# A diffusion trunk with experts: weight rows read in pieces of 8 KB

## The chip, the cores and the metric

The kernel runs on one core of a Trainium2 chip. The metric is the time on the device in microseconds, the median of several executions. Before the change it is 2671.46 us (three runs, 2670.12 to 2673.77).

## The reference

Two layers of a diffusion backbone work on 512 latent tokens and 256 context tokens of width 1024, all in float32. A layer first mixes tokens in four parallel branches, and then sends each token through two of 16 experts. The change lies in this second half:

```python
h2 = modulate(rms_norm(x, norm2_g[i]), m[:, 3], m[:, 4])
x = x + m[:, 5] * grouped_moe(h2, router_w, router_b, moe_w1[i], moe_w3[i], moe_w2[i])
...
def grouped_moe(h, router_w, router_b, w1, w3, w2):
    logits = jnp.einsum('bld,de->ble', h, router_w, preferred_element_type=jnp.float32)
    ...
    for e in range(N_EXPERTS):
        a = jax.nn.silu(h @ w1[e]) * (h @ w3[e])
        y = y + combine[..., e:e + 1] * (a @ w2[e])
    return y
```

`w1[e]` and `w3[e]` are 1024 x 256, `w2[e]` is 256 x 1024: 1 MiB each; `combine` holds for each token the weights of its two experts, both of one group, and zeros. Layer 0 treats 768 tokens, layer 1 only the 512 latent ones.

## The kernel before, in words

There are 128 partitions (P), and D = 1024 = KD x P with KD = 8. Each engine has its own program; semaphores order them. The order of the work is written out by hand.

**Modulation.** The kernel begins with 48 slabs of 1 MiB of the modulation matrices, which SyncE loads into six slots (five in RING, one in HTF), each partition in eight pieces of 1 KB. During this time GpSimd loads constants, among them `rwv`, the router weights.

**Mixers.** For each layer there follow attention, the gating MLP, the convolution, the pooling and the output projection, in matmuls of L569 and L571. SyncE loads their weights into RAWB; ScalarE and VectorE split them into two parts.

**Router.** When the last column chunk of the output projection is in `x_t`, VectorE makes the modulated tokens, one tile of 128 tokens at a time: L1626 multiplies by the inverse norm and the gain, L1627 adds the shift, both over 128 x 1024 elements, into one of three buffers `h2tok`. Layer 0 has six tiles, layer 1 four. Of each tile ScalarE stores the rows to `h2_rows` in HBM (L1218). TensorE transposes it in eight pieces of 128 columns (L838, into `psb`), ScalarE copies the result to `h2T` (L1222), and eight products with the router weights `rwv[:, k, :]` follow (L846). TensorE takes the tiles in turn: transposes of tile t + 1, then the products of tile t. Piece k of a tile holds the columns k x 128 to k x 128 + 127, and `rwv` partition p holds rows k x 128 + p.

Then VectorE picks the experts in some 40 short instructions. Three of them (L1642, L1643, L1644) add pairs of the four scores of each group and write them to a table that has six columns for each group: L1642 writes runs of three elements, L1643 runs of two, L1644 single elements, so that the runs of one instruction lie 24 B apart. Products on TensorE give each token its place (L858 to L868). The result is a list of blocks: 27 blocks of 128 rows in layer 0 and 23 in layer 1, each with one expert (`eid_i`), and for each block the tokens that it gathers (`tab_i`).

**Experts.** For block b:

- GpSimd gathers 128 rows of `h2_rows` into `xg[b % 2]` (L1888), two blocks ahead; TensorE transposes them in eight pieces (L877) and ScalarE copies the result to `xgT` (L1240).
- SyncE loads three slabs of 1 MiB, `w1`, `w3` and `w2` of the block's expert, into the next of the six slots (L466), as soon as the slot is released (`slab_used`). In `w1` and `w3` partition p receives the rows p, p + 128, ..., eight pieces of 1 KB; in `w2` the rows p and p + 128, two pieces of 4 KB.
- TensorE multiplies (L885): for both matrices the sum over k of `xgT[:, k, :]` by `slot[:, k, :]`, 128 x 256 results each.
- ScalarE applies the silu to the first (L1236), VectorE multiplies it by the second into `act_a` (L1723), TensorE transposes `act_a` in two pieces (L901), and ScalarE copies them to `act_T` (L1244).
- TensorE multiplies by `w2` (L894), one block later; VectorE copies the result out (L1729), and ScalarE stores it to `y_rows` (L1249).

TensorE's order for a block is: L885 of block b, L877 of block b + 1, L894 of block b - 1, L901 of block b. After the last block GpSimd waits for the stores and gathers each token's two rows from `y_rows` (L1910); before it, it has issued the parameter loads of the next layer (L1808 to L1823).

Of the kernel before, what the change touches and what calls it, by code (L numbers as in the profile page):

```python
# [21 lines left out]
ALU = mybir.AluOpType  # L22
# [3 lines left out]
P = 128  # L26
D = 1024
KD = D // P
# [31 lines left out]
FF = 256  # L60
# [83 lines left out]
def trunk(nc, A, out):  # L144
# [7 lines left out]
    with ExitStack() as ctx:  # L152
# [3 lines left out]
        def place(name, width, dt=F32, parts=P, over=None):  # L156


            at_ = free[0] if over is None else over
            if over is None:  # L160
                free[0] += (width + 7) // 8 * 8
            return nc.alloc_sbuf_tensor_at(name, [parts, width], dt, offset=base + 4 * at_)
# [25 lines left out]
        rst = place("rst", 2 * AT)  # L188
# [15 lines left out]
        def W(l):  # L204
            return TOK if l < DEPTH - 1 else SEQ
# [4 lines left out]
        x_t = X[:, :].rearrange("p (t d) -> p t d", t=AT)  # L210
# [27 lines left out]
        def slot(s):  # L238
            return RING[:, s * SLAB:(s + 1) * SLAB] if s < SLOTS - 1 else HTF[:, 8 * D:8 * D + SLAB]
# [4 lines left out]
        def psb(i):  # L244
            return ps[:, i, :]
# [63 lines left out]
        mrow = HTF[:, 0:4 * D].rearrange("p (v m d) -> p v m d", v=2, m=2)  # L309
        gain2 = HTF[:, 4 * D:5 * D]  # L310
        grow = T[:, 0:2 * D].rearrange("p (v d) -> p v d", v=2)
        h2tok = [BRA[:, j * D:(j + 1) * D] for j in range(3)]
# [6 lines left out]
        sil = [late[:, 2 * D + j * FF:2 * D + (j + 1) * FF] for j in range(2)]  # L319
        act_a = [late[:, 2 * D + (2 + j) * FF:2 * D + (3 + j) * FF] for j in range(2)]  # L320
# [45 lines left out]
        rwv = rw[:, :].rearrange("p (k e) -> p k e", k=KD)  # L366
# [16 lines left out]
        def S(name):  # L383
            if name not in sems:
                sems[name] = ctx.enter_context(nc.semaphore(name))
            return sems[name]

        def at(name, l, n):

            return n + (signals(name) if l else 0)  # L390
# [64 lines left out]
        @block.sync  # L455
        def _(sp):
            issued = [0]

            def load(shape, src, before=None, at=None):

                n = issued[0] if at is None else at
                if n >= SLOTS or before is not None:
                    need = n - SLOTS + 1
                    sp.wait_ge(slab_used, need if before is None else before + need)
                a, m = shape
                sp.dma_start(slot(n % SLOTS)[:, 0:a * m].rearrange("p (a m) -> p a m", a=a), src)\  # L466
                    .then_inc(slab_full[n % SLOTS], 16)
                if at is None:
                    issued[0] += 1


            def mod_cols(l, c0):
                return A["mod_w"][l][:, c0].rearrange("(k p) n -> p k n", p=P)

            for j in range(SLOTS):
                load((KD, 256), mod_cols(0, slice(j * 256, (j + 1) * 256)))
            for l in range(DEPTH):
                start = 1 if l == 0 else 0
                turn0 = l * MC // 2
                with sp.Fori(start, MC // (2 * SLOTS)) as i:  # L480
                    for j in range(SLOTS):
                        load((KD, 256), mod_cols(l, bass.ds(i * (256 * SLOTS) + j * 256, 256)), i * SLOTS, turn0 + j)
                issued[0] = (l + 1) * MC // 2

            for l in range(DEPTH):

                if l == 0:
                    sp.wait_ge(S("mod_row"), DEPTH * MC // 2)
                else:
                    sp.wait_ge(S("y_sb"), at("y_sb", l - 1, expert_blocks(W(l - 1))))  # L490
                for r, pieces in enumerate(loads[l]):
                    if RAWS <= r < FIRST + 1:
                        sp.wait_ge(S("w_lo"), at("w_lo", l, r - RAWS + 1))
                    elif FIRST + 1 <= r < FIRST + RAWS:
                        sp.wait_ge(S("up_sb"), at("up_sb", l, up_items(l, AT)))
                    elif r >= FIRST + RAWS:
                        sp.wait_ge(S("w_lo"), split_no(l, r - FIRST - RAWS))
                    for o, a, m, src in pieces:
                        sp.dma_start(raw_slab(r, RAW)[:, o:o + a * m].rearrange("p (a m) -> p a m", a=a), src)\
                            .then_inc(raw_full[r % RAWS], 16)  # L500
                nb = expert_blocks(W(l))
                w1, w3, w2 = A["moe_w1"][l], A["moe_w3"][l], A["moe_w2"][l]

                sp.wait_ge(S("eid"), at("eid", l, 1))

                def up(b, n, before=None):
                    e = sp.value_load(eid_i[0:1, b] if before is None else eid_i[0:1, bass.ds(b, 1)],
                                      min_val=0, max_val=NE - 1)
                    for w in (w1, w3):
                        load((KD, FF), w[bass.ds(e, 1)].rearrange("e (k p) n -> p (e k) n", p=P), before, n)  # L510
                        n = None if n is None else n + 1

                def down(b, n, before=None):
                    e = sp.value_load(eid_i[0:1, b] if before is None else eid_i[0:1, bass.ds(b, 1)],
                                      min_val=0, max_val=NE - 1)
                    load((2, D), w2[bass.ds(e, 1)].rearrange("e (k p) n -> p (e k) n", p=P), before, n)

                up(slice(0, 1), None)

                sp.wait_ge(S("idx"), at("idx", l, 2))  # L520
                for b in (1, 2):
                    up(slice(b, b + 1), None)
                    down(slice(b - 1, b), None)
                n0 = issued[0]
                with sp.Fori(0, (nb - 3) // 2) as i:
                    for j in range(2):
                        up(i * 2 + (3 + j), n0 + 3 * j, i * SLOTS)
                        down(i * 2 + (2 + j), n0 + 3 * j + 2, i * SLOTS)
                issued[0] += 3 * (nb - 3)
                down(slice(nb - 1, nb), None)  # L530

            sp.wait_ge(S("x_stored"), 16 * LT)
# [750 lines left out]
        def _(dve):  # L1283
            chain = [0]

            def link(ins):

                chain[0] += 1
                ins.then_inc(S("dve_chain"), 1)
                dve.wait_ge(S("dve_chain"), chain[0])  # L1290

            tt, ts, stt, cp = dve.tensor_tensor, dve.tensor_scalar, dve.scalar_tensor_tensor, dve.tensor_copy
# [15 lines left out]
            for l in range(DEPTH):  # L1308
                n = l * MC // 2
# [48 lines left out]
            for l in range(DEPTH):  # L1358
# [104 lines left out]
                for n in range(len(steps) + 3):  # L1463
                    if n < len(steps):
                        h, t = steps[n]
# [12 lines left out]
                    if 2 <= n <= len(steps) + 1:  # L1478
                        m = n - 2
                        h, t = steps[m]  # L1480
# [4 lines left out]
                    if n >= 3:  # L1485
                        m = n - 3
                        h, t = steps[m]
# [46 lines left out]
                for c in range(BC):  # L1534
                    w = 3 * c + 2
# [39 lines left out]
                for g in range(BC):  # L1575
# [5 lines left out]
                    src, lo, k = pp[g % 2], 1, 1  # L1581
# [3 lines left out]
                    while 2 * k < win_:  # L1585
                        link(tt(pacc[1 - cur][:, lo + k:hi - k], pacc[cur][:, lo:hi - 2 * k], pacc[cur][:, lo + 2 * k:hi], ALU.add))
                        cur, lo, hi, k = 1 - cur, lo + k, hi - k, 2 * k
                    s_ = pacc[cur]
                    e = edge[:, (BC - 1 - g) * 2 * PP:(BC - g) * 2 * PP]
                    for a, b, o in pstreams:  # L1590
                        n = b - a
# [29 lines left out]
                for t in range(NT):  # L1621
                    v = 0 if t < LT else 1
                    if t >= 3:
                        dve.wait_ge(S("h2_tr"), at("h2_tr", l, t - 2))
                        dve.wait_ge(S(f"h2_st{t % 3}"), at(f"h2_st{t % 3}", l, 16 * (t // 3)))
                    link(stt(h2tok[t % 3], x_t[:, t, :], rst[:, t:t + 1], mrow[:, v, 1, :], ALU.mult, ALU.mult))  # L1626
                    tt(h2tok[t % 3], h2tok[t % 3], mrow[:, v, 0, :], ALU.add).then_inc(S("h2_tok"), 1)  # L1627


                s, sbv, m_, sc = (a[:, 0:NT, :] for a in (r_s, r_sb, r_m, r_sc))  # L1630
# [88 lines left out]
                def hidden(b, j, first=False):  # L1719
                    dve.wait_ge(S("sil"), at("sil", l, b + 1))  # L1720
                    if not first:
                        dve.wait_ge(S("aT_ps"), at("aT_ps", l, b - 1))
                    tt(act_a[j], sil[j], psb(1)[:, FF:2 * FF], ALU.mult).then_inc(S("a_sb"), 1)  # L1723

                def rows_out(b, j, stored=None):
                    dve.wait_ge(S("y_ps"), at("y_ps", l, b + 1))
# [21 lines left out]
                for t in range(NT + 3):  # L1748
                    if t < NT:
                        v = 0 if t < LT else 1  # L1750
# [12 lines left out]
        def _(pool):  # L1763
            chain = [0]

            def link(ins):

                chain[0] += 1
                ins.then_inc(S("pool_chain"), 1)
                pool.wait_ge(S("pool_chain"), chain[0])  # L1770
# [11 lines left out]
            for l in range(DEPTH):  # L1782
                for v in range(2):
                    pool.dma_start(mod_sb[l][v:v + 1, :], A["mod_b"][l].rearrange("(a n) -> a n", a=1)).then_inc(S("mod_b"), 16)
            pool.dma_start(rwv, A["router_w"].rearrange("(k p) e -> p k e", p=P)).then_inc(S("const_dma"), 16)
            pool.dma_start(rbias[:, :], A["router_b"].rearrange("(a e) -> a e", a=1).partition_broadcast(P)).then_inc(S("const_dma"), 16)
            pool.dma_start(edge[:, :], A["edges"].rearrange("g e -> (g e)").rearrange("(a n) -> a n", a=1).partition_broadcast(P))\
                .then_inc(S("const_dma"), 16)
# [47 lines left out]
            for l in range(DEPTH):  # L1836
# [67 lines left out]
                for t in range(NT):  # L1904
                    j = t % 3
# [29 lines left out]
```

## Time and profile before

| | |
|---|---|
| median of three runs | 2671.46 us (2670.12 to 2673.77) |
| span of the profiled execution | 2674.0 us; no time beside its span is given |
| TensorE matmuls busy | 2344.6 us, 88% |
| TensorE weight loads busy | 1882.4 us, 70% |
| VectorE busy | 1057.0 us, 40% |
| ScalarE busy | 746.3 us, 28% |
| DMA | 397.74 MB in 358022 packets |
| expert weights, SyncE's queue | 150 loads of 1024 KB, 7.5 us from issue to landing (median) |

The page gives for each engine the busy time and, in 40 equal slices of the span, its busy share in tenths. The stretches of the expert stages are about 1240 to 1560 us (layer 0) and 2370 to 2644 us (layer 1). The busy end of a matmul is modelled, so what TensorE waits for is read from the chain of waits and from the idle time that the timeline prints in brackets, with what ended it.

### The profile page before, as it was taken

How to read it: one execution, taken by the hardware profiler on the slowest of the kernel's cores; microseconds unless marked ns; L12 is line 12 of the kernel's file. 1: busy time of each engine (PE TensorE's matmuls, PEld its weight loads, DVE VectorE, ACT ScalarE, POOL GpSimd, SP SyncE). 2: the span in 40 equal slices, each digit the busy share in tenths (PEclk: the TensorE clock that was granted, in tenths of full speed). 3: DMA queues.
4: the chain of work that ended last, by engine and by line, in shares of the span. 5: the costliest groups of instructions: out<-in, count | busy, mean ns of one | idle time of the engine just before them, and what ended most of it. 6: DMA issues, size and time to landing. Idle time of an engine off the chain costs nothing.

```text
span 2674.0 us, 31031 instructions
## 1 busy us (share of the span) xinstructions
PE 2344.6 (88%) x12289; PEld 1882.4 (70%) x12289; DVE 1057.0 (40%) x1455; ACT 746.3 (28%) x1086; POOL 152.8 (6%) x231
## 2 busy tenths in 40 slices
PE   6877599999999999976999936599999999869995
PEld 4555478888888888865777725388878777657773
DVE  5782777213224243232111153675243454321113
ACT  4552444214112122231111132443232222311111
POOL 1010200000000000000101120200000000001111
PEclk9988799999999999987999977799999999879998
DMA  9970100122122223215999971100233433269996
GB/s 329 355 236 1 48 1 1 44 55 71 48 60 76 59 68 99 81 57 196 361 369 364 368 279 34 47 1 24 76 94 83 110 91 127 83 227 365 366 367 227
DMA packets 358022, 397.74 MB, mean 149 GB/s; under 512 B 9852, under 2 KB 319260, under 8 KB 356892
## 3 DMA queue, kind: packets, MB, share of 16 engines
q1 hardware_dynamic: 331264, 297.56, 35.8%
q0 software_dynamic: 14272, 53.63, 5.6%
q10 hardware_dynamic: 12384, 45.09, 4.2%
q8 instruction: 75, 1.23, 0.2%
q14 instruction: 27, 0.22, 0.0%
HBM read 359.45 MB, written 36.80 MB: 148 GB/s over the span
## 4 chain that ended last, share of the span: by engine, by line
PE 56%; DVE 6%; ACT 2%; issue 1%; DMA 1%; POOL 0%; POOLq 0%; DVEq 0%; ACTq 0%
PE ps L569 22%; PE ps L885 13%; PE ps L894 6%; PE ps L571 4%; PE ps L559 3%; PE ps L877 2%; PE ps L741 2%; PE ps L730 1%; PE ps L846 1%; DMA MGZ<-y_rows,slot_i 1%; ACT BR L1213 0%; DVE X L1392 0%; PE ps L901 0%; PE ps L838 0%; PE ps L700 0%
## 5 line engine op out<-in xcount | busy, mean ns | idle before, releaser
L569 PE MATMUL ps<-HTH,WS 128*128 128x512 f32 x1664 | 581.2, 396 | 15.1 <-issue 7.3
L569 PEld LDWEIGHTS ps<-HTH,WS 128*128 128x128 f32 x1664 | 314.2, 189 | 88.5 <-issue 9.9
L569 PE MATMUL ps<-HTL,WS 128*128 128x512 f32 x832 | 327.6, 394 | 0.0
L1420 DVE TENSOR_TENSOR WS<-RAWB,WS 128x1024 fp32r<-128x1024 f32 (+1 forms) x128 | 190.5, 1490 | 222.7 <-ACT WS L1071 222.3
L885 PE MATMUL ps<-RING,MGZ 128*128 128x256 f32 x1216 | 275.9, 384 | 2.8 <-ACT MGZ L1240 2.8
L885 PEld LDWEIGHTS ps<-RING,MGZ 128*128 128x128 f32 x1216 | 232.5, 193 | 35.4 <-ACT MGZ L1240 3.9
L1071 ACT ACTIVATE WS<-RAWB 128x1024 fp32r<-128x1024 f32 (+1 forms) x128 | 162.6, 1272 | 263.0 <-PE ps L571 133.3
L571 PE MATMUL ps<-HTH,WS 128*128 128x256 f32 x832 | 233.2, 280 | 0.0
L569 PE MATMUL ps<-BRH,WS 128*128 128x512 f32 x512 | 183.2, 396 | 6.5 <-DVE BRL L1572 3.6
L569 PEld LDWEIGHTS ps<-HTL,WS 128*128 128x128 f32 x832 | 157.2, 189 | 36.0 <-issue 0.7
L894 PE MATMUL ps<-RING,MGZ 128*128 128x512 f32 x392 | 176.4, 593 | 0.5 <-ACT MGZ L1244 0.5
L1437 DVE TENSOR_TENSOR T<-T,ps 128x768 f32<-128x768 f32 (+1 forms) x48 | 39.4, 820 | 312.7 <-PE ps L571 202.0
L1723 DVE TENSOR_TENSOR MGZ<-MGZ,ps 128x256 f32<-128x256 f32 x50 | 21.1, 421 | 348.5 <-ACT MGZ L1236 348.5
L571 PEld LDWEIGHTS ps<-HTH,WS 128*128 128x128 f32 x832 | 157.5, 189 | 0.1
L1089 ACT ACTIVATE T<-ps 128x768 f32<-128x768 f32 (+1 forms) x64 | 45.1, 705 | 302.8 <-PE ps L571 190.0
L559 PE MATMUL ps<-MODH,scH 128*2 128x256 f32 x384 | 110.0, 286 | 21.3 <-DVE MODL L1301 20.3
L1729 DVE COPY MGZ<-ps 128x1024 f32<-128x1024 f32 x50 | 61.2, 1224 | 170.4 <-PE ps L894 170.4
L894 PEld LDWEIGHTS ps<-RING,MGZ 128*128 128x128 f32 x392 | 70.7, 190 | 71.0 <-issue 70.3
L569 PEld LDWEIGHTS ps<-BRH,WS 128*128 128x128 f32 x512 | 96.7, 189 | 30.1 <-DVE BRL L1572 4.8
L571 PE MATMUL ps<-HTL,WS 128*128 128x256 f32 x416 | 116.3, 280 | 0.0
L1236 ACT ACTIVATE MGZ<-ps 128x256 f32<-128x256 f32 x50 | 19.2, 384 | 334.6 <-PE ps L885 334.6
L559 PE MATMUL ps<-MODL,scH 128*2 128x256 f32 x384 | 109.9, 286 | 0.0
(295 smaller groups left out, 3892.8 us busy)
## 6 DMA issues: line engine op xcount, KB each, us to landing
RING<-in_moe_w SPq DMA_DIRECT2D x125, 1024.0 KB, 7.5
RAWB<-in_w_in SPq DMA_DIRECT2D x112, 512.0 KB, 3.9
RING<-in_mod_w SPq DMA_DIRECT2D x40, 1024.0 KB, 11.7
HTF<-in_moe_w SPq DMA_DIRECT2D x25, 1024.0 KB, 7.4
y_rows<-MGZ ACTq DMA_DIRECT2D x50, 512.0 KB, 6.9
RAWB<-in_w_branch SPq DMA_DIRECT2D x64, 256.0 KB, 4.4
HTF<-in_mod_w SPq DMA_DIRECT2D x8, 1024.0 KB, 11.8
RAWB<-in_w_o SPq DMA_DIRECT2D x16, 512.0 KB, 3.6
```

What stands on the lines that cost most here:

```text
L559: last = mm(out, a, b, start=(first and i == 0), stop=(stop and i == 2))
L569: last = mm(psb(pair)[:, 0:SEQ], a[:, k0 + k, :], b[:, k, 0:SEQ], start=go, stop=end)
L571: last = mm(psb(pair)[:, SEQ:TOK], a[:, k0 + k, :], b[:, k, SEQ:TOK], start=go, stop=end)
L741: last = mm(psb(3)[0:VD, (m % 2) * P:(m % 2 + 1) * P], vb[:, kt, h * VD:(h + 1) * VD], prT[m % 2][:, kt * P:(kt + 1) * P], start=(kt == ks ...
L877: last = pe.transpose(psb(0)[:, k * P:(k + 1) * P], xg[j][:, k * P:(k + 1) * P], ident[:, :])
L885: last = mm(psb(1)[:, o:o + FF], xgT[j][:, k, :], slot3(s, KD)[:, k, :], start=(k == 0), stop=(k == KD - 1))
L894: last = mm(psb(2 + j)[:, n * 512:(n + 1) * 512], act_T[j][:, k, :], w[:, k, n * 512:(n + 1) * 512], start=(k == 0), stop=(k == 1))
L1071: act_f(parts(s, words(s))[0], raw_slab(r, words(s)), ACT.Copy).then_inc(S("w_hi"), 1)
L1089: act_f(sig[u % 2][:, 0:W(l)], psb(u % 2)[:, 0:W(l)], ACT.Sigmoid).then_inc(S("g_sig"), 1)
L1420: tt(lo, raw_slab(FIRST + s, words(s)), hi.bitcast(F32), ALU.subtract).then_inc(S("w_lo"), 1)
L1437: link(tt(prod[:, 0:W(l)], sig[u % 2][:, 0:W(l)], psb(2 + u % 2)[:, 0:W(l)], ALU.mult))
L1729: cp(ysb[j], psb(2 + j)).then_inc(S("y_sb"), 1)
```

## The change

Partition p of the expert weights now receives consecutive rows: the rows 8p to 8p + 7 of `w1` and `w3`, and the rows 2p and 2p + 1 of `w2`. Both are one piece of 8 KB for each partition. What is multiplied by them must stand in the same order: piece k of a tile of tokens must hold the columns 8p + k. For this L1626 and L1627 write column 8p + k to place k x 128 + p; what they read from `x_t` and `mrow` stays in order, and L1627 reads its first operand where it writes it. `h2_rows` and the gathered rows then have this order without more work. The router weights are loaded in it too. L1723 does the same for `w2` with two pieces.

```diff
@@ experts, SyncE @@
                     for w in (w1, w3):
-                        load((KD, FF), w[bass.ds(e, 1)].rearrange("e (k p) n -> p (e k) n", p=P), before, n)
+                        load((KD, FF), w[bass.ds(e, 1)].rearrange("e (p k) n -> p (e k) n", p=P), before, n)
...
-                    load((2, D), w2[bass.ds(e, 1)].rearrange("e (k p) n -> p (e k) n", p=P), before, n)
+                    load((2, D), w2[bass.ds(e, 1)].rearrange("e (p k) n -> p (e k) n", p=P), before, n)
@@ tokens, VectorE @@
-                    link(stt(h2tok[t % 3], x_t[:, t, :], rst[:, t:t + 1], mrow[:, v, 1, :], ALU.mult, ALU.mult))
-                    tt(h2tok[t % 3], h2tok[t % 3], mrow[:, v, 0, :], ALU.add).then_inc(S("h2_tok"), 1)
+                    by_row = h2tok[t % 3].rearrange("q (k p) -> q p k", k=KD)
+
+                    def rows_of(a):
+                        return a.rearrange("q (p k) -> q p k", k=KD)
+
+                    link(stt(by_row, rows_of(x_t[:, t, :]), rst[:, t:t + 1], rows_of(mrow[:, v, 1, :]), ALU.mult, ALU.mult))
+                    tt(by_row, by_row, rows_of(mrow[:, v, 0, :]), ALU.add).then_inc(S("h2_tok"), 1)
@@ gated product, VectorE @@
-                    tt(act_a[j], sil[j], psb(1)[:, FF:2 * FF], ALU.mult).then_inc(S("a_sb"), 1)
+                    tt(act_a[j].rearrange("q (k p) -> q p k", k=2), sil[j].rearrange("q (p k) -> q p k", k=2),
+                       psb(1)[:, FF:2 * FF].rearrange("q (p k) -> q p k", k=2), ALU.mult).then_inc(S("a_sb"), 1)
@@ constants, GpSimd @@
-            pool.dma_start(rwv, A["router_w"].rearrange("(k p) e -> p k e", p=P)).then_inc(S("const_dma"), 16)
+            pool.dma_start(rwv, A["router_w"].rearrange("(p k) e -> p k e", p=P)).then_inc(S("const_dma"), 16)
```

## Rows read from the trace of the kernel before

**Rows 1.** The page: TensorE's busy time; DMA share and rate in 40 slices.

```profile
PE 2344.6 (88%) x12289; PEld 1882.4 (70%) x12289; DVE 1057.0 (40%) x1455; ACT 746.3 (28%) x1086; POOL 152.8 (6%) x231
...
DMA  9970100122122223215999971100233433269996
GB/s 329 355 236 1 48 1 1 44 55 71 48 60 76 59 68 99 81 57 196 361 369 364 368 279 34 47 1 24 76 94 83 110 91 127 83 227 365 366 367 227
```

**Rows 2.** The page: the chain of waits, share of the span by line.

```profile
PE ps L569 22%; PE ps L885 13%; PE ps L894 6%; PE ps L571 4%; PE ps L559 3%; PE ps L877 2%; PE ps L741 2%; PE ps L730 1%; PE ps L846 1%; DMA MGZ<-y_rows,slot_i 1%; ACT BR L1213 0%; DVE X L1392 0%; PE ps L901 0%; PE ps L838 0%; PE ps L700 0%
```

**Rows 3.** The chain in order of time (start us, us), layer 0's experts.

```profile
1269.89 6.91 PE ps L885 x32
...
1532.93 6.91 PE ps L885 x32
```

**Rows 4.** Waits of SyncE's queue, 1269 to 1537 us: total, times, longest.

```profile
SPq L466 <- PE ps L901: 76.9, 24, 3.3
```

**Rows 5.** DMA, 130 to 155 us: modulation slabs in pieces of 1 KB.

```profile
DMA packets 8633, 8.70 MB, mean 348 GB/s; under 512 B 136, under 2 KB 8633, under 8 KB 8633
```

**Rows 6.** DMA, 1525 to 1562 us: rate in 40 slices, packets by size.

```profile
GB/s 403 421 412 360 376 369 343 348 356 369 384 381 394 421 412 421 443 412 430 412 412 403 406 318 188 177 319 421 415 328 241 98 0 0 244 403 407 80 0 0
DMA packets 4621, 11.77 MB, mean 318 GB/s; under 512 B 432, under 2 KB 2512, under 8 KB 4365
```

**Rows 7.** TensorE's timeline (start, us, [idle before]), start of both expert stages.

```profile
1243.79 1.94 PE L877 MATMUL ps<-ident,BR 128*128 128x128 f32 x8 [6.10 <-DMA BR<-h_rows,idx_i]
1246.84 9.36 PE L885 MATMUL ps<-RING,MGZ 128*128 128x256 f32 x32 [1.11 <-ACT MGZ L1240]
...
2375.47 9.95 PE L885 MATMUL ps<-RING,MGZ 128*128 128x256 f32 x32 [1.11 <-ACT MGZ L1240]
```

**Rows 8.** By stretch: busy us by engine, granted clock (PEclk), DMA share, GB/s.

```profile
1246.80:1251.50 4.70, 4.66 (x11) 3.75 (x12) 0.00 (x0) 1.28 (x1) 0.97 (x1) 0.52 1.01 356
```

**Rows 9.** GpSimd's timeline, end of layer 0.

```profile
1566.14 1.06 POOL L1910 DMA_INDIRECT MGZ<-y_rows,slot_i  x1 [15.26 <-DMA y_rows<-MGZ]
```

**Rows 10.** Timelines of VectorE and TensorE in one block, 1400 to 1424 us.

```profile
1403.22 0.42 DVE L1723 TENSOR_TENSOR MGZ<-MGZ,ps 128x256 f32<-128x256 f32 x1 [6.49 <-ACT MGZ L1236]
...
1403.31 3.60 PE L894 MATMUL ps<-RING,MGZ 128*128 128x512 f32 x8
1406.75 0.38 PE L901 MATMUL ps<-ident,MGZ 128*128 128x128 f32 x2
```

**Rows 11.** TensorE's timeline, router: tiles 1, 2 and 5 of layer 0, tile 3 of layer 1.

```profile
1193.72 1.97 PE L838 MATMUL ps<-ident,BR 128*128 128x128 f32 x8 [0.47 <-DVE BR L1627]
...
1197.98 1.09 PE L838 MATMUL ps<-ident,BR 128*128 128x128 f32 x8
...
1206.60 1.09 PE L838 MATMUL ps<-ident,BR 128*128 128x128 f32 x8
...
2340.47 1.09 PE L838 MATMUL ps<-ident,BR 128*128 128x128 f32 x8
```

**Rows 12.** VectorE's timeline, tiles 2 and 5 of layer 0, tile 3 of layer 1.

```profile
1194.90 1.22 DVE L1627 TENSOR_TENSOR BR<-BR,HTF 128x1024 f32<-128x1024 f32 x1
...
1202.29 1.23 DVE L1627 TENSOR_TENSOR BR<-BR,HTF 128x1024 f32<-128x1024 f32 x1
...
2336.56 1.23 DVE L1627 TENSOR_TENSOR BR<-BR,HTF 128x1024 f32<-128x1024 f32 x1
```

**Rows 13.** VectorE's groups by form: count, busy us, mean ns, idle before.

```profile
L1627 DVE TENSOR_TENSOR BR<-BR,HTF 128x1024 f32<-128x1024 f32 x10 | 12.2, 1225 | 0.3
L1612 DVE TENSOR_TENSOR X<-X,ps 128x768 f32<-128x768 f32 x8 | 7.6, 954 | 46.5 <-PE ps L825 46.5
...
L1642 DVE TENSOR_TENSOR BR<-BR 128x72 f32<-128x72 f32 x1 | 0.2, 234 | 0.0
L1642 DVE TENSOR_TENSOR BR<-BR 128x48 f32<-128x48 f32 x1 | 0.2, 210 | 0.0
L1644 DVE TENSOR_TENSOR BR<-BR 128x24 f32<-128x24 f32 x1 | 0.2, 194 | 0.0
L1644 DVE TENSOR_TENSOR BR<-BR 128x16 f32<-128x16 f32 x1 | 0.2, 181 | 0.0
```

## The prediction

> **What bounds the kernel now.** I read the page first. TensorE is busy 88% of the span, and 16 DMA engines are nearly full in three stretches: the modulation matrices at the start and the expert stage of each layer [rows 1]. The change touches the expert stages, so the question is which of the two ends last there. The chain of waits over the whole span gives the expert lines L885 and L894 13% and 6% as TensorE work, and no weight load stands among its lines [rows 2].
>
> The slices show the difficulty: there the DMA engines are full too, at 361 to 369 GB/s in the whole slices. The chain in order of time settles it. One block of 128 rows is 32 matmuls of L885 and what follows them (8 transposes, 8 matmuls of L894, 2 transposes), and in the middle of layer 0's stage it comes back 23 times in (1532.93 - 1269.89)/23 = 11.44 us, each time the 6.91 us of L885 and no transfer between them [rows 3]. From the other side, SyncE waits on TensorE for a slab to be freed, 24 times and 76.9 us in the largest of three such groups [rows 4]; no row has TensorE waiting for a weight slab. So the loads are hidden, but only just: a block moves 3 MiB of weights, 0.5 MiB of gathered rows and 0.5 MiB of results, 4.19 MB in 11.44 us = 367 GB/s.
>
> **The loads: what 8 KB pieces change.** With nothing but 1 KB pieces the engines are full at about 348 GB/s: the modulation stage [rows 5]. Where 4 KB and 8 KB pieces mix with them, behind the last gather of layer 0 (256 packets of 8 KB are in that window), single slices run at 400 to 443 GB/s [rows 6]. Now half of a block's bytes (w1, w3) go in 1 KB pieces: 2.10 MB / 348 = 6.0 us; the other half in 4 KB pieces at some 410: 5.1 us; together 11.1 of the 11.44 us. After the change 4.19 MB / 410 = 10.2 us. The gain of 0.9 us a block is worth nothing, because TensorE's 11.44 us cover either number: 46 blocks in the steady state, 0 us. Were that cover gone, the 0.9 us would be worth 41 us. From the other side, a loss begins only where pieces of 8 KB flow at under 367 GB/s.
>
> The Trainium skill, "DMA: Bandwidth & Descriptors", section "Why small descriptors are slow (HBM only)", gives each packet about 3 extra bus cycles of 32 bytes. That is 35 against 32 for 1 KB and 259 against 256 for 8 KB, so by it 348 would become some 376 GB/s, an estimate from that page. The slices of [rows 6] already exceed it, and by either number the sum does not move.
>
> Where the loads are not in the steady state: block 0 of layer 0 starts at 1246.84, behind the first gather, its transposes and their copy. Its 9.36 us for 32 matmuls instead of 6.91 are the granted clock, 0.52 (the lower level, 1.2 GHz) up to 1251.5, and not a late slab; layer 1 has 9.95 us there [rows 7, 8]. TensorE does wait for the first gather, 6.10 us in layer 0 [rows 7]. Its packets come to an end while the next weight loads begin, and those now stand in front of it in 8 KB packets instead of 1 KB. 16 engines at 367 GB/s need 0.36 us for one, so one or two of them cost 0 to 0.7 us a layer; for two layers I take +0.4 us. It can gain no more than the same.
>
> At the end of a layer nothing is lost: after the next layer's parameter loads, which share the engines with the last weights, GpSimd still waits 15.26 us for the last results to be stored [rows 9], so they may land that much later. The router weights (512 B rows instead of 64 B) load during the modulation stage and L846 first reads them behind tile 1's transposes, after 1193.72 us [rows 11]: 0.
>
> **The gated product (L1723).** 50 instructions of 0.42 us, now written with a step of 512 B between consecutive elements. In the steady state it ends at 1403.64 and the transposes that read it start at 1406.75, behind the 3.6 us of L894 [rows 10]: 3.1 us of cover, seven times its length. Block 0 has no L894 in front, but there TensorE waits for ScalarE's copy of the next gathered rows anyway. I take 0. Without the cover even a doubling would cost 0.27 us x 50 = 13 us.
>
> **The tokens (L1626, L1627).** Here the change is on the path. These two instructions make one tile of h2. TensorE waits for the first two tiles of a layer (tile 1 of layer 0: 0.47 us) and for none after them: a tile takes TensorE (1206.60 - 1197.98)/3 = 2.87 us in L838 and L846, VectorE (1202.29 - 1194.90)/3 = 2.46 us [rows 11, 12]. From there to block 0 everything is a chain (router, one-hots, table, gather), so a delay of the last router matmul arrives in full. Let each of the two instructions become x longer. In layer 0 tile t is ready 2x(t+1) later. Tiles 0 and 1 have no slack; tile 2 has 1197.98 - 1196.12 = 1.8 us, and tile 5 has 1206.60 - 1203.52 = 3.0. The end is later by the largest of 4x (tile 1) and 12x - 3.0 (tile 5). In layer 1, with four tiles and 2340.47 - 2337.79 = 2.6 us of slack at tile 3, it is the largest of 4x and 8x - 2.6.
>
> What is x? No row has an instruction that steps by 512 B. The nearest are the pair sums of the router, whose results step by 24 B from one group to the next [rows 13]. Runs of three elements cost (234 - 210)/24 = 1.0 ns an element, as in contiguous rows, (1225 - 954)/256 = 1.06. Single elements cost (194 - 181)/8 = 1.63. The surplus of 0.57 ns over 1024 elements is x = 0.58 us. Below: x = 0, as stepping rows of three elements cost nothing. Above: a second full slot for each element, x = 1.09 us. I take 0.58, the row of single elements, as that is the new pattern. Then layer 0: max(2.3, 4.0) = 4.0; layer 1: max(2.3, 2.0) = 2.3. Sum with the gather: 4.0 + 2.3 + 0.4 = **+6.7 us**.
>
> The durations come from an execution with a span of 2674.0 us, for which no time beside its span is given; that is 0.1% above the median of 2671.46 of the three runs, to which I add the sum: 2678.2.
>
> **Rivals.**
> 1. *Stepping is free* (x = 0). For: the rows of three elements, and what L1626 only reads stays contiguous. Against: single elements differ. Sum 0 to +0.4: 2671.6 us.
> 2. *A full second slot*, x = 1.09: layer 0 13.1 - 3.0 = 10.1, layer 1 8.7 - 2.6 = 6.1, sum 16.6: 2688 us. For it speaks only that 512 B is far beyond 24 B. If only L1627, which also reads at that step, pays it, the sum is 3.5 + 2.2 + 0.4: 2677.6, beside my number for another reason. The Trainium skill, "Advanced Engine Details and Errata", section "SBUF Cachelines", says that full speed needs at least two accesses to the same line of 16 bytes; it names no price. The order of the two prices, for runs of three and for single elements, agrees with it; no row shows it at this step.
> 3. *Faster*: the start of the expert stage is waiting for weights after all, and block 0's surplus, 9.36 - 6.91 and 9.95 - 6.91, goes. That is 2.45 + 3.04 = 5.5 us, which with free stepping gives 2666. Against it stands the clock of 0.52 [rows 8]. It decides only if x is next to 0.
> 4. *Pieces of 8 KB are slower than 1 KB*, below 367 GB/s: each GB/s below costs 0.03 us a block; at the 348 of [rows 5] it is 12.0 - 11.44 = 0.6 us x 46 = +28 us: 2699. Against: the slices of [rows 6].
>
> **How the numbers follow.** 0.2% of this kernel, 5.3 us, is about what a measurement can tell from no change; x above about 0.5 passes it. Chances: my case (x from 0.3 to 0.8) 0.40, of it 0.30 above the bound and 0.10 within; free stepping 0.33; the second slot 0.17; faster 0.07; slower loads 0.03. Slower 0.30 + 0.17 + 0.03 = 0.50; same 0.10 + 0.33 = 0.43; faster 0.07. The range leaves out rivals 3 and 4 and a little of the edges: 2670 to 2689; my own case alone spans 2673 to 2682.
>
> **What the profile would show.** L1627 near 1.81 instead of 1.23 us and L1626 longer by as much; the waits of L838 on L1627 longer by 1 to 2 us; block 0 starting 4 us later in layer 0; L1723 perhaps longer without effect; the interval of 11.44 us unchanged; DMA packets down by 50 x 2048 x 7/8 and 50 x 128 = 96,000; a DMA share in the expert stage that falls from 1.03 to about 0.9. I am wrong if the interval moves, if L1627 keeps its 1.23 us, or if TensorE gets new idle time there that keeps its clock low for longer.

## The result, and the profile after

Compared in turns on one chip, the changed kernel took 2683.25 us (9 runs, 2678.72 to 2687.82) and the kernel before 2673.77 us (9 runs, 2670.12 to 2683.04): ratio 1.0031, 95% interval 1.0020 to 1.0042. By the ratio that is 8.3 us more (interval 5.3 to 11.2), where 6.7 were forecast. The median of the kernel before lay between 2673.8 and 2678.2 us over all comparisons, so below only the ratios of runs made together are compared.

First the groups of VectorE by form (count | busy us, mean ns | idle before) of the changed kernel; L1631, L1632 and L1728 are L1626, L1627 and L1723 of the kernel before. L1627 stands in [rows 13]; the first two lines here are the other two of the kernel before:

```profile
L1626 DVE SCALAR_TENSOR_TENSOR BR<-X,rst,HTF 128x1024 f32<-128x1024 f32 x10 | 12.8, 1280 | 0.1
L1723 DVE TENSOR_TENSOR MGZ<-MGZ,ps 128x256 f32<-128x256 f32 x50 | 21.1, 421 | 348.5 <-ACT MGZ L1236 348.5
...
L1728 DVE TENSOR_TENSOR MGZ<-MGZ,ps 128x256 f32<-128x256 f32 x50 | 30.4, 608 | 348.2 <-ACT MGZ L1236 348.2
L1631 DVE SCALAR_TENSOR_TENSOR BR<-X,rst,HTF 128x1024 f32<-128x1024 f32 x10 | 19.9, 1992 | 0.1
L1632 DVE TENSOR_TENSOR BR<-BR,HTF 128x1024 f32<-128x1024 f32 x10 | 19.2, 1918 | 0.3
```

L1632 is 1918 - 1225 = 693 ns longer than L1627, and L1631 is 1992 - 1280 = 712 ns longer than L1626. The gated product, 421 ns before, is 187 ns longer over 256 elements, 0.73 ns an element. So the step costs about 0.7 us in an instruction of 1024 elements.

What TensorE makes of it stands in its timeline, changed kernel, router of layer 0 and then layer 1 (start, us, idle before), to be held against [rows 11]:

```profile
1190.30 1.94 PE L838 MATMUL ps<-ident,BR 128*128 128x128 f32 x8 [13.85 <-DVE BR L1632]
1194.10 1.97 PE L838 MATMUL ps<-ident,BR 128*128 128x128 f32 x8 [1.86 <-DVE BR L1632]
...
1198.30 1.10 PE L838 MATMUL ps<-ident,BR 128*128 128x128 f32 x8
...
1201.86 1.10 PE L838 MATMUL ps<-ident,BR 128*128 128x128 f32 x8 [0.61 <-DVE BR L1632]
...
1205.72 1.09 PE L838 MATMUL ps<-ident,BR 128*128 128x128 f32 x8 [0.92 <-DVE BR L1632]
...
1209.60 1.09 PE L838 MATMUL ps<-ident,BR 128*128 128x128 f32 x8 [0.93 <-DVE BR L1632]
...
1215.17 0.54 PE L852 MATMUL ps<-ident,MGZ 16*128 16x16 f32 x6 [0.89 <-ACT MGZ L1224]
...
2339.28 1.97 PE L838 MATMUL ps<-ident,BR 128*128 128x128 f32 x8 [1.86 <-DVE BR L1632]
2341.18 3.20 PE L846 MATMUL ps<-MGZ,rw 128*16 128x128 f32 x16
...
2347.19 1.09 PE L838 MATMUL ps<-ident,BR 128*128 128x128 f32 x8
...
2352.55 0.42 PE L852 MATMUL ps<-ident,MGZ 16*128 16x16 f32 x4 [0.68 <-ACT MGZ L1224]
```

In layer 0 tiles 3, 4 and 5 now wait for VectorE, which they did not before: VectorE has become the slower of the two, at 3.9 us a tile. In layer 1 only tiles 0 and 1 wait. To measure the stage I take the reciprocal (L1620), which comes just before the first tile, as its start, and the transposes of the router's scores (L852) as its end. VectorE's rows of the changed kernel:

```profile
1186.09 0.19 DVE L1620 RECIPROCAL rst<-srt 128x6 f32<-128x6 f32 x1 [1.35 <-ACT srt L1215]
...
2331.27 0.18 DVE L1620 RECIPROCAL rst<-srt 128x4 f32<-128x4 f32 x1 [1.35 <-ACT srt L1215]
```

and five rows of the kernel before that are not shown above, VectorE's and TensorE's:

```profile
1188.44 0.19 DVE L1620 RECIPROCAL rst<-srt 128x6 f32<-128x6 f32 x1 [1.35 <-ACT srt L1215]
...
1212.18 0.54 PE L852 MATMUL ps<-ident,MGZ 16*128 16x16 f32 x6 [0.89 <-ACT MGZ L1224]
...
2327.66 0.18 DVE L1620 RECIPROCAL rst<-srt 128x4 f32<-128x4 f32 x1 [1.35 <-ACT srt L1215]
...
2334.83 2.84 PE L846 MATMUL ps<-MGZ,rw 128*16 128x128 f32 x16
...
2345.84 0.42 PE L852 MATMUL ps<-ident,MGZ 16*128 16x16 f32 x4 [0.68 <-ACT MGZ L1224]
```

Layer 0: (1215.17 - 1186.09) - (1212.18 - 1188.44) = 5.3 us. Layer 1: 21.28 - 18.18 = 3.1 us. Together 8.4 us, as much as the ratio gives (8.3 us).

These are rows of one execution each, and the granted clock does not rise at the same moment in all of them. The changed kernel once more (last experiment) shows it in the first products of layer 0:

```profile
1198.33 3.60 PE L846 MATMUL ps<-MGZ,rw 128*16 128x128 f32 x16
```

They take 3.60 us at a granted clock of 0.50, instead of 2.37 us at 0.79; tiles 3 and 4 then do not wait, and still its stage lasts 29.07 us, where the profile above has 29.08: VectorE sets the end. In executions where VectorE's instructions have their old length, TensorE sets it, and the stage of layer 0 lasts between 23.5 (2.17 us for these products) and 25.2 us (3.60 us). So the 5.3 us of layer 0 are known to about 1.5 us.

The loads did change. The chain of waits of the changed kernel, first and last of 24 blocks, and the table by stretch (busy us by engine, granted clock, DMA share, GB/s) show what became of it:

```profile
1284.56 6.91 PE ps L885 x32
...
1547.60 6.91 PE ps L885 x32
```

```profile
1280.00:1550.00 270.00, 270.00 (x1181) 202.52 (x1180) 44.00 (x48) 43.03 (x72) 34.16 (x60) 1.00 0.97 367
```

The interval is (1547.60 - 1284.56)/23 = 11.44 us, as in [rows 3]. The DMA engines move the same 367 GB/s with a share of 0.97 (about 0.9 was forecast), where the same stretch of the kernel before has 1.03:

```profile
1270.00:1540.00 270.00, 270.00 (x1185) 203.88 (x1184) 38.77 (x47) 41.52 (x71) 34.12 (x60) 1.00 1.03 366
```

The packets fell from 358,022 to 262,022, by the 96,000 of the forecast.

### The profile page after: what moved, and what is told of

It reads as the page before. It is cut to its first block, busy times and chain, and to the rows that moved or that the text cites. A ratio compares the mean times of both kernels' runs of the same rounds, so it can differ in the third digit from the quotient of the medians.

```text
span 2681.4 us, 31031 instructions
## 1 busy us (share of the span) xinstructions
PE 2344.2 (87%) x12289; PEld 1880.6 (70%) x12289; DVE 1080.1 (40%) x1455; ACT 746.6 (28%) x1086; POOL 152.4 (6%) x231
## 2 busy tenths in 40 slices
DMA packets 262022, 397.74 MB, mean 148 GB/s; under 512 B 9852, under 2 KB 216860, under 8 KB 241692
## 3 DMA queue, kind: packets, MB, share of 16 engines
q8 instruction: 75, 1.23, 0.2%
## 4 chain that ended last, share of the span: by engine, by line
PE 56%; DVE 7%; ACT 2%; issue 2%; DMA 1%; POOL 0%; POOLq 0%; DVEq 0%; ACTq 0%
PE ps L569 22%; PE ps L885 13%; PE ps L894 6%; PE ps L571 4%; PE ps L559 3%; PE ps L877 2%; PE ps L741 2%; PE ps L730 1%; DMA MGZ<-y_rows,slot_i 1%; DVE BR L1631 1%; PE ps L846 0%; ACT BR L1213 0%; DVE X L1392 0%; PE ps L901 0%; DVE BR L1632 0%
## 5 line engine op out<-in xcount | busy, mean ns | idle before, releaser
L885 PE MATMUL ps<-RING,MGZ 128*128 128x256 f32 x1216 | 276.5, 385 | 2.7 <-ACT MGZ L1240 2.7
L885 PEld LDWEIGHTS ps<-RING,MGZ 128*128 128x128 f32 x1216 | 233.0, 193 | 35.4 <-ACT MGZ L1240 3.7
L1728 DVE TENSOR_TENSOR MGZ<-MGZ,ps 128x256 f32<-128x256 f32 x50 | 30.4, 608 | 348.2 <-ACT MGZ L1236 348.2
L1735 DVE COPY MGZ<-ps 128x1024 f32<-128x1024 f32 x50 | 61.2, 1225 | 161.8 <-PE ps L894 154.9
```

The source lines that it names most:

```text
L885: last = mm(psb(1)[:, o:o + FF], xgT[j][:, k, :], slot3(s, KD)[:, k, :], start=(k == 0), stop=(k == KD - 1))
L1735: cp(ysb[j], psb(2 + j)).then_inc(S("y_sb"), 1)
```

## The experiments

**The loads alone.** The two lines of SyncE are changed, all else is the kernel before. The products then pair tokens and weights that do not belong together.

```diff
-  w[bass.ds(e, 1)].rearrange("e (k p) n -> p (e k) n", p=P)
+  w[bass.ds(e, 1)].rearrange("e (p k) n -> p (e k) n", p=P)      # w1, w3, and w2 likewise
```

> The kernel before with only SyncE's expert loads changed to 8 KB pieces (the products then pair tokens and weights in different orders). My theory: TensorE's 11.44 us per block hide them, so the interval stays 11.44 us, and the ratio to before is 1.000 within 0.0005. Rival (8 KB packets delay other traffic, such as the first gather or the stores, and this is part of the 0.31%): ratio above 1.001. Rival (a gain that the token part hides): below 0.999.

Ratio 0.9993, interval 0.9983 to 1.0003. The interval of a block is 11.44 us. In the table by stretch of this kernel the only clear difference is the DMA share, 0.98 instead of 1.03:

```profile
1270.00:1540.00 270.00, 270.00 (x1181) 202.41 (x1181) 38.27 (x47) 42.61 (x72) 34.10 (x60) 1.00 0.98 366
```

A gain of up to 0.17% is not excluded; a loss above 0.03% is. The loads carry none of the 0.31%.

**VectorE alone.** The changed kernel with the old loads (the diff above, backwards).

> The changed kernel with SyncE's expert loads put back to 1 KB and 4 KB pieces (the products then pair tokens and weights in different orders); the stepping writes of VectorE and the router weights stay. My theory: the whole loss is here, ratio to before 1.003 (1.002 to 1.004), L1631 at 1.99 us and L1632 at 1.92, router stage later by 5.3 us in layer 0 and 3 us in layer 1. Rival (the loads carry part of it): ratio 1.001 or less.

Ratio 1.0022, interval 1.0014 to 1.0031; the groups by form are those of the changed kernel:

```profile
L1631 DVE SCALAR_TENSOR_TENSOR BR<-X,rst,HTF 128x1024 f32<-128x1024 f32 x10 | 19.9, 1995 | 0.1
L1632 DVE TENSOR_TENSOR BR<-BR,HTF 128x1024 f32<-128x1024 f32 x10 | 19.2, 1921 | 0.3
```

The loss is here. The interval overlaps that of the whole change (1.0020 to 1.0042), and the stage, measured as above, lasts 29.12 us in layer 0 and 21.28 in layer 1, as in the changed kernel (29.08 and 21.28).

**The cover taken away.** Both kernels with half of the products of w1 and w3 left out; all loads stay.

```diff
-  for k in range(KD):
+  for k in range(KD // 2):
       last = mm(psb(1)[:, o:o + FF], xgT[j][:, k, :], slot3(s, KD)[:, k, :],
-                start=(k == 0), stop=(k == KD - 1))
+                start=(k == 0), stop=(k == KD // 2 - 1))
```

> The kernel before, with L885 summing only four of the eight pieces (half of the products of w1 and w3 are left out, all loads stay). TensorE then needs 11.44 - 16 x 0.216 = 8.0 us a block, and no longer covers the DMA engines. My theory, from 2.10 MB at 348 GB/s and 2.10 MB at 410: the interval becomes 11.1 us, set by the loads. Rival (1 KB pieces are not the limit and the engines follow TensorE): 8 to 10 us.

> The changed kernel with the same half of the products left out. My theory: interval 10.2 us (4.19 MB at 410 GB/s), 0.9 us a block less than with the small pieces, so 46 x 0.9 = 41 us less in the expert stages, and against the other kernel with half the products some 33 us after the loss of the tokens. Rival (packet size does not matter to these loads): the same interval in both.

Small pieces: ratio 0.9903 to the kernel before (0.9880 to 0.9927), median 2655.65 us. Pieces of 8 KB: 0.9717 (0.9701 to 0.9734), 2603.54 us. The first answer is that of the small pieces, TensorE's waits and the table by stretch, the second that of the 8 KB pieces:

```profile
PE ps L885 <- DMA RING<-in_moe_w: 45.5, 21, 4.0
...
1280.00:1500.00 220.00, 181.25 (x666) 123.16 (x667) 32.58 (x40) 35.41 (x59) 23.08 (x40) 0.90 1.06 380
```

```profile
PE ps L885 <- DMA RING<-in_moe_w: 45.2, 24, 6.7
...
1280.00:1500.00 220.00, 182.84 (x756) 124.39 (x757) 40.29 (x44) 39.38 (x66) 30.41 (x54) 1.00 1.02 422
```

Now L885 waits for the slabs in both, and the rate is what the DMA engines can give: 380 GB/s in small pieces, 422 in 8 KB pieces. With 4.19 MB that is 11.0 and 9.9 us a block (forecast 11.1 and 10.2). The 1.1 us a block, 51 us over 46 blocks, are the gain of the 8 KB pieces, and it appears only where TensorE does not cover it. Between the two medians lie 2655.65 - 2603.54 = 52 us, where 33 were forecast. The loss of the tokens, 8 us, is already taken off there, so the loads gave about 60 us, 9 more than the 51. The clock may be part of that: with small pieces TensorE was granted 0.90 in the stretch, with large ones 1.00. No run separates the two. Rival 4, slower large pieces, is out.

**Which step costs, in writes.** The changed kernel with the old loads and another permutation in each tile of layer 0, so that consecutive elements are written 8, 16, 32, 128, 512 and 2048 B apart in tiles 0 to 5. The columns stand in a wrong order.

```diff
-  by_row = h2tok[t % 3].rearrange("q (k p) -> q p k", k=KD)
+  kk = (512, 256, 128, 32, 8, 2)[t]
+  by_row = h2tok[t % 3].rearrange("q (k p) -> q p k", k=kk)      # and so in rows_of
```

> The changed kernel with the old loads, and with another step for the writes of the two token instructions in each tile: 8, 16, 32, 128, 512 and 2048 B for tiles 0 to 5 (the columns then stand in another order in each tile). Theory A (a write that does not stay in a 16 B line costs, whatever the step): 1.28 and 1.23 us at 8 B, 1.99 and 1.92 us at all steps from 16 B on. Theory B (the cost grows with the step, as the row at 24 B with 0.57 ns and the result at 512 B with 0.70 suggest): rising from 8 B to 2048 B. Theory C (only steps of large powers of two cost): full speed at 16 and 32 B.

VectorE's timeline, tiles 0 (8 B), 1 (16 B), 4 (512 B) and 5 (2048 B); in this kernel and the next, L1632 and L1633 are L1626 and L1627 of the kernel before:

```profile
1187.69 1.28 DVE L1632 SCALAR_TENSOR_TENSOR BR<-X,rst,HTF 128x1024 f32<-128x1024 f32 x1
1189.01 1.23 DVE L1633 TENSOR_TENSOR BR<-BR,HTF 128x1024 f32<-128x1024 f32 x1
1190.16 2.07 DVE L1632 SCALAR_TENSOR_TENSOR BR<-X,rst,HTF 128x1024 f32<-128x1024 f32 x1
1192.26 1.97 DVE L1633 TENSOR_TENSOR BR<-BR,HTF 128x1024 f32<-128x1024 f32 x1
...
1202.18 2.05 DVE L1632 SCALAR_TENSOR_TENSOR BR<-X,rst,HTF 128x1024 f32<-128x1024 f32 x1
1204.26 1.92 DVE L1633 TENSOR_TENSOR BR<-BR,HTF 128x1024 f32<-128x1024 f32 x1
1206.09 2.04 DVE L1632 SCALAR_TENSOR_TENSOR BR<-X,rst,HTF 128x1024 f32<-128x1024 f32 x1
1208.16 2.01 DVE L1633 TENSOR_TENSOR BR<-BR,HTF 128x1024 f32<-128x1024 f32 x1
```

Theory A holds: 8 B are free, 16 B cost the full price, and 2048 B no more. Tiles 2 and 3 (32 and 128 B) take 2.07 and 2.00 us in L1632, 2.02 and 2.09 in L1633. The price does not grow with the step, so 512 B was no special case. This is one execution, and the four tiles of its layer 1 repeat the first four within 0.02 us. All these steps are powers of two; others were not measured, but for the 24 B of the router's rows.

**Which step costs, in reads.** The same, walking in the written order: the writes are contiguous, L1632 reads two operands with the step, L1633 one (the shift; its other operand is contiguous).

```diff
+  kk = (2, 4, 8, 32, 128, 512)[t]
+  by_row = h2tok[t % 3].rearrange("q (k p) -> q k p", k=kk)      # and so in rows_of
```

> The same with contiguous writes and the steps in what is read, 2048, 1024, 512, 128, 32 and 8 B for tiles 0 to 5 counted by the elements of x and mrow: L1631 reads two stepping operands, L1632 one (columns in another order in each tile). Theory A (only writes pay): 1.28 and 1.23 us everywhere. Theory B (reads pay as writes do): 1.99 and 1.92 us for all but the 8 B tile, and more in L1631 if both operands count.

The expectation has the steps in the wrong order: they are 8, 16, 32, 128, 512 and 2048 B in tiles 0 to 5. Again this is one execution. Tiles 0, 1, 4 and 5:

```profile
1183.36 1.28 DVE L1632 SCALAR_TENSOR_TENSOR BR<-X,rst,HTF 128x1024 f32<-128x1024 f32 x1
1184.68 1.22 DVE L1633 TENSOR_TENSOR BR<-BR,HTF 128x1024 f32<-128x1024 f32 x1
1185.83 2.07 DVE L1632 SCALAR_TENSOR_TENSOR BR<-X,rst,HTF 128x1024 f32<-128x1024 f32 x1
1187.93 1.98 DVE L1633 TENSOR_TENSOR BR<-BR,HTF 128x1024 f32<-128x1024 f32 x1
...
1197.98 2.47 DVE L1632 SCALAR_TENSOR_TENSOR BR<-X,rst,HTF 128x1024 f32<-128x1024 f32 x1
1200.49 1.91 DVE L1633 TENSOR_TENSOR BR<-BR,HTF 128x1024 f32<-128x1024 f32 x1
1202.30 1.33 DVE L1632 SCALAR_TENSOR_TENSOR BR<-X,rst,HTF 128x1024 f32<-128x1024 f32 x1
1203.67 1.24 DVE L1633 TENSOR_TENSOR BR<-BR,HTF 128x1024 f32<-128x1024 f32 x1
```

Reads pay like writes from 16 B on. With two stepping operands L1632 takes 2.07, 2.10, 2.19 and 2.47 us at 16, 32, 128 and 512 B, so there the price does grow with the step. Tile 5 is the odd one: its walk takes one element here, one 2048 B further on, the next one here, and so on. Read in this way it costs almost nothing; written in the same way (tile 5 of the writes) it costs the full price.

**The step moved into the reads.** The same result as the changed kernel; `"q (k p) -> q k p"` and `"q (p k) -> q k p"` in the places of the patterns of the diff.

> The changed kernel with the same result, but each of the three instructions walks in the order in which it writes, so the writes are contiguous and the reads step (32 B in the tokens, 8 B in the gated product). If reads do not pay: L1631 and L1632 back at 1.28 and 1.23 us, ratio to before 1.000, 8 us less than the changed kernel. If they pay as writes do: ratio 1.003 as the changed kernel.

Ratio 1.0042, interval 1.0029 to 1.0056. L1631 and L1632 take 2094 and 2010 ns, more than with stepping writes; the gated product, which reads with a step of 8 B, is back at 421 ns. It is the expectation's second case. The stage lasts 30.30 us in layer 0 and 21.90 in layer 1, so in the trace it is somewhat worse than the changed kernel (29.08 and 21.28); the intervals of the two ratios overlap.

**One instruction instead of two.** L1633 (L1626 of the kernel before) writes contiguously to a free buffer, only L1634 writes with the step.

```diff
-  link(stt(by_row, rows_of(x_t[:, t, :]), rst[:, t:t + 1], rows_of(mrow[:, v, 1, :]), ALU.mult, ALU.mult))
-  tt(by_row, by_row, rows_of(mrow[:, v, 0, :]), ALU.add).then_inc(S("h2_tok"), 1)
+  if t:
+      dve.wait_ge(S("h2_tok"), at("h2_tok", l, t))
+  link(stt(junk, x_t[:, t, :], rst[:, t:t + 1], mrow[:, v, 1, :], ALU.mult, ALU.mult))
+  tt(by_row, rows_of(junk), rows_of(mrow[:, v, 0, :]), ALU.add).then_inc(S("h2_tok"), 1)
```

> The changed kernel with the same result, but L1631 writes contiguously to a buffer that is free at this time, and only L1632 writes with the step. L1631 back at 1.28 us, L1632 stays at 1.92; a tile costs 0.7 us more than before instead of 1.4. By the sum of the prediction: layer 0 max(1.4, 4.2 - 3.0) = 1.4, layer 1 max(1.4, 2.8 - 2.6) = 1.4, together 2.8 us: ratio to before 1.001. Rival (the read at the step of 512 B is what pays in L1632): L1632 back near 1.23 us and ratio 1.000.

```profile
L1634 DVE TENSOR_TENSOR BR<-BR,HTF 128x1024 f32<-128x1024 f32 x10 | 19.4, 1935 | 0.3
L1633 DVE SCALAR_TENSOR_TENSOR BR<-X,rst,HTF 128x1024 f32<-128x1024 f32 x10 | 12.8, 1285 | 0.7
```

Ratio 1.0016, interval 1.0004 to 1.0027: half of the cost, 4.3 us, where 2.8 were forecast. L1634 reads contiguously here and still takes 1935 ns, so the write alone costs the full price. The stage grows by 2.2 us in layer 0 and 2.4 in layer 1 instead of 1.4 each. What is beyond the forecast stands in the first products of each layer, which the sum had left out: they take 2.98 and 3.60 us, 2.42 and 2.84 before.

**Pairs.** As in the last one, but the walk of L1634 and of the gated product takes two elements in a row wherever it writes, and reads two lines by turns.

```diff
-  by_row = h2tok[t % 3].rearrange("q (k p) -> q p k", k=KD)
+  by_row = h2tok[t % 3].rearrange("q (k u i) -> q u k i", k=KD, i=2)
...
-      return a.rearrange("q (p k) -> q p k", k=KD)
+      return a.rearrange("q (u i k) -> q u k i", k=KD, i=2)
```

> The changed kernel with the same result and its 8 KB loads, but VectorE walks so that two elements in a row share a line of 16 B wherever it writes: L1633 goes contiguously to the free buffer, L1634 and the gated product write pairs (pairs 512 B apart), and read two lines by turns, one element of each. Theory (the price is for a write that has its line of 16 B alone, and reads of two lines by turns cost nothing, as tile 5 of the read steps with 1.33 and 1.24 us has it): L1634 near 1.25 us, gated product near 0.42 us, ratio to before 1.000, 8 us less than the changed kernel. Rival (any jump of 512 B costs, pair or not): L1634 near 1.6 to 1.9 us, ratio 1.001 to 1.002.

```profile
L1730 DVE TENSOR_TENSOR MGZ<-MGZ,ps 128x256 f32<-128x256 f32 x50 | 21.1, 422 | 348.7 <-ACT MGZ L1236 348.7
L1634 DVE TENSOR_TENSOR BR<-BR,HTF 128x1024 f32<-128x1024 f32 x10 | 12.4, 1238 | 0.3
```

Ratio 0.9996, interval 0.9987 to 1.0005: the same permutation, the same 8 KB pieces, and the cost is gone. The jump of 512 B is still there after each pair, and the instruction takes 1238 ns instead of 1225. (L1633 takes 1285 ns, as in the last experiment; the walk in pairs was not tried in it.)

**The step on TensorE.** Tokens and gated product stay in order as before; the transposes read with the step.

```diff
-  h2tok[t % 3][:, k * P:(k + 1) * P]
+  h2tok[t % 3].rearrange("q (p k) -> q k p", k=KD)[:, k, :]      # and so for xg (k=KD) and act_a (k=2)
```

> The changed kernel with the same result and its 8 KB loads, but tokens and gated product stay in plain order, VectorE as in the kernel before, and TensorE's transposes read with the step (32 B in L838 and L877, 8 B in L901). If TensorE's reads at a step are free: transposes at 0.11 us each, interval 11.44 us, ratio 1.000. If they pay as VectorE's do (0.7 of a slot per element): 10 transposes of some 0.11 us grow to 0.19 us, interval 12.2 us, +0.8 us x 48 = +38 us, ratio 1.014.

TensorE's timeline of this kernel, one block:

```profile
1409.87 1.05 PE L877 MATMUL ps<-ident,BR 128*128 128x128 f32 x8
...
1414.19 0.39 PE L901 MATMUL ps<-ident,MGZ 128*128 128x128 f32 x2
```

Ratio 0.9991, interval 0.9982 to 1.0000. The eight transposes of L877 take 1.05 us instead of 1.04, those of L838 1.16 instead of 1.09, and the interval of a block is 11.46 us. The step is not free for TensorE itself: it stands in the loads of the weights, which run beside the matmuls. TensorE's groups of weight loads, this kernel and then the kernel before (count, busy us, mean ns, idle before):

```profile
L877 PEld LDWEIGHTS ps<-ident,BR 128*128 128x128 f32 x416 | 55.5, 192 | 16.0 <-issue 13.3
...
L877 PEld LDWEIGHTS ps<-ident,BR 128*128 128x128 f32 x416 | 49.9, 144 | 17.1 <-issue 12.1
```

A load takes 192 ns instead of 144 with a step of 32 B, and 197 instead of 141 in L901 with a step of 8 B, but almost nothing of it reaches the time of the transposes.

**The changed kernel again**, with these last two:

> The changed kernel once more, on the same chip as the two others: ratio 1.003 as before, so that their differences are not those of a chip.

Ratio 1.0032, interval 1.0021 to 1.0042. Its interval does not touch those of the two versions that write in pairs or step on TensorE. Neither of these is shown to beat the kernel before: what they keep of the change, the faster loads, is covered.

## Why the prediction was right

- **The bound of the expert stage** was read rightly: the interval stayed at 11.44 us, the loads alone gave 0.9993, and with the cover gone they gave 1.1 us a block (0.9 forecast). Both were priced a little high: the small pieces at 11.1 us against 11.0, the large ones at 10.2 against 9.9.
- **The place of the loss** was right: L1626 and L1627 on the path, with two tiles without slack and the last tile deciding in layer 0.
- **x was sized too low**: 0.58 us, from two rows of single elements that differ by 13 ns, against 0.69 in L1632 and 0.71 in L1631. No row said that a price read at a step of 24 B would hold even roughly at 512 B. The write steps showed it only afterwards, so this part was luck. With 0.70 the formulas give 12 x 0.70 - 3.0 = 5.4 us for layer 0 (measured 5.3) and the larger of 4 x 0.70 = 2.8 and 8 x 0.70 - 2.6 = 3.0 for layer 1. In layer 1 3.1 us came, but by the other way: tile 3 does not wait, the products after tiles 0 and 1 start 2.7 us later and take 3.20 us instead of 2.84, the rest. They run while the granted clock changes between its levels; it was 0.57 over them, 0.66 before. The prediction named this effect and did not price it. That the longer wait in front keeps the clock low is not shown. In layer 1 the products take 3.17 to 3.21 us in three executions with this wait (1.86 us), and 2.81 to 2.91 in four with a wait of at most 0.60. But with a wait of 1.30 us (one instruction instead of two) they take 3.60, and with 2.07 (the step moved into the reads) 3.03.
- **The gather's +0.4 us is not seen.** TensorE waits 5.90 and 5.83 us for it, instead of 6.10 and 5.76. But the changed kernel again has 6.11 and 6.30, so single executions differ by more than the term, and no run shows it or excludes it.
- **The sum**: 4.0 + 2.3 + 0.4 = 6.7 us against 5.3 + 3.1 and no gather. The two layers were priced 2.1 us too low, and the unseen 0.4 hides a little of that. Of the 5 us between the 2678.2 that were forecast and 2683.25, 2.3 are the kernel before, which was measured at 2673.77 instead of 2671.46.
- **Rival 1**, free stepping, fell in its general form, but it is true for a step of 8 B and for pairs. **Rival 2**, a full second slot of 1.09 us, was too dear; the price is 0.7. **Rival 3** had no place: with 8 KB pieces the 32 matmuls of block 0 of layer 0 still take 9.80 us, with a granted clock of 0.50 over the first half.
- **The gated product** grew to 608 ns, as unimportant as was said: TensorE waits for it 0.23 us in block 0 of each layer, in place of a wait for ScalarE's copy.
- The Trainium skill, "Advanced Engine Details and Errata", section "SBUF Cachelines", asks for at least two accesses to a line of 16 B. For writes the runs agree: two to a line are enough (8 B step, pairs), one is not (16 B step and up). For reads they agree but for one kind: reads that change lines at every element and come back to both are nearly free (tile 5 of the read steps, 1.33 and 1.24 us; L1634 of the pairs, 1238 ns).
- The Trainium skill, "DMA: Bandwidth & Descriptors", section "Why small descriptors are slow (HBM only)", gave the estimate of 376 GB/s from 348. No run here has a stage of 8 KB weight pieces alone. The mixed stage went from 380 to 422, a factor of 1.11 where the estimate has 1.08 with all bytes in 1 KB pieces to begin with, so by the runs it is too small.

## What to carry to other kernels

Before a load is made faster, ask what covers it, and find the price of the order that it forces on others: here a covered gain of 1.1 us a block was bought with 0.7 us in instructions on the path. If a permutation must be made, walk so that elements are written in pairs of neighbours, or let TensorE's transpose read with the step; both took the loss away here, and neither made the kernel faster than before. And look at the pace of both engines in a pipeline of tiles: later tiles may have slack, but once the feeding engine becomes the slower one (3.9 us a tile against 2.87), each further tile adds.

## What had not been expected of the hardware

- VectorE's price for float32 writes at steps of 16, 32, 128, 512 and 2048 B is 0.67 to 0.84 ns an element and does not grow with the step (2.07 against 1.28 us and 1.97 against 1.23 at 16 B, 2.04 and 2.01 at 2048 B), and not a second slot of 1.06.
- Reads of two places by turns, 2048 B apart and each going on by 4 B, take 1.24 us instead of 1.22, writes of that kind 2.01: only the times are shown, the mechanism is not.
- Two operands read with a step of 512 B cost 2.47 us, one 1.91. Why these two lie further apart at 512 B than at 16 B (2.07 and 1.98) stays open.
- TensorE's weight loads do pay for a step, and at 8 B already, which is free on VectorE: 197 instead of 141 ns at 8 B, 192 instead of 144 at 32 B. The eight transposes around them take 1.05 instead of 1.04 us.
